# A two-layer encoder step: gathered expert rows of the early steps scaled by ScalarE and added by GpSimd

## What is computed

```
q     = (xn @ w_q).reshape(T, 8 heads, 2, 128)
sc    = q . sub_keys                    # two lists of 128 scores per head
top_s, top_i = top_k(sc, 16)            # best keys of each list
best_s, sel  = top_k(all 16*16 sums, 16); idx = pairs of keys   # choice of 16 experts
gate  = softmax(best_s)
act   = gelu(exp_u[idx] . xn)           # one dot product per chosen expert
y     = sum over heads, k of gate * act * exp_v[idx]
```

## Time and profile before

| what | value |
|---|---|
| median of 3 runs | 3265.97 us |
| the profiled execution's own time | 3254.12 us |
| its span, first to last instruction | 3252.3 us |
| granted TensorE clock, mean | 0.935 of full |
| PE busy | 2958.9 us (91%) |
| DVE busy | 2473.6 us (76%) |
| ACT busy | 811.2 us (25%) |
| POOL busy | 1056.1 us (32%) |
| DMA | 1042.99 MB, mean 321 GB/s |
| chain that ended last | PE 40%, DMA 40%, DVE 11%, issue 7% |

### The profile page before, as it was taken

The page is one execution under the profiler, slowest core; times in us unless marked ns, Lnnn a source line. Parts: engine busy times, 40 slices in busy tenths (PEclk is TensorE's granted clock), DMA queues, the critical chain, the costliest instruction groups (busy, mean ns, idle before and its releaser), DMA issues.

```text
span 3252.3 us, 46708 instructions
## 1 busy us (share of the span) xinstructions
PE 2958.9 (91%) x17310; PEld 2582.9 (79%) x17310; DVE 2473.6 (76%) x5433; ACT 811.2 (25%) x2388; POOL 1056.1 (32%) x840
## 2 busy tenths in 40 slices
PE   6898989999999999967878978789999999999876
PEld 6797778888888888855666957678888888888755
DVE  2366799988888888877533776898888888888876
ACT  4332222212111111211354362222112111112111
POOL 4532122333333333333354321122333323333331
PEclk8999999999999999988877968889999999999988
DMA  5336778999999999999311257678999999999995
GB/s 163 96 97 246 262 273 322 360 421 422 422 422 420 415 416 421 407 422 416 131 58 52 97 194 266 229 262 311 420 421 422 422 422 418 419 417 417 406 421 200
DMA packets 159967, 1042.99 MB, mean 321 GB/s; under 512 B 18480, under 2 KB 23920, under 8 KB 44096
## 3 DMA queue, kind: packets, MB, share of 16 engines
q0 software_dynamic: 92160, 671.13, 50.8%
q1 hardware_dynamic: 63648, 357.59, 28.5%
q10 hardware_dynamic: 4000, 12.36, 1.1%
HBM read 1033.28 MB, written 7.86 MB: 320 GB/s over the span
## 4 chain that ended last, share of the span: by engine, by line
PE 40%; DMA 40%; DVE 11%; issue 7%; POOL 1%; ACT 1%; SPq 0%; DVEq 0%; ACTq 0%; POOLq 0%
DMA gata<-uvg,idxg 24%; DMA gatb<-uvg,idxg 15%; PE bank L713 11%; PE bank L516 8%; DVE acc L1600 5%; PE bank L726 4%; PE bank L503 3%; PE bank L700 3%; PE bank L505 3%; PE bank L504 3%; PE bank L602 1%; PE bank L533 1%; PE bank L860 1%; DVE gata L1592 1%; PE bank L838 1%
## 5 line engine op out<-in xcount | busy, mean ns | idle before, releaser
L726 PE MATMUL bank<-a,V 128*128 128x256 f32 x4096 | 947.8, 392 | 102.5 <-DVE a L1583 102.5
L726 PEld LDWEIGHTS bank<-a,V 128*128 128x128 f32 x4096 | 805.3, 197 | 229.0 <-issue 112.6
L713 PE MATMUL bank<-xd,U 128*128 128x256 f32 x4096 | 940.2, 389 | 0.0
L1273 POOL DMA_INDIRECT gata<-uvg,idxg x428 | 525.9, 1229 | 1236.2 <-DVE acc L1600 1176.8
L713 PEld LDWEIGHTS bank<-xd,U 128*128 128x128 f32 x4096 | 790.3, 195 | 107.7 <-issue 0.2
L1592 DVE CUSTOM_DVE_ANT_0 gata<-gata,xrow 128x1024 f32<-128x1024 f32 x428 | 522.9, 1222 | 201.7 <-DMA gata<-uvg,idxg 194.9
L1600 DVE SCALAR_TENSOR_TENSOR acc<-gata,wgt,acc 128x1024 f32<-128x1024 f32 x428 | 548.5, 1281 | 32.6 <-ACT wgt L1085 32.5
L1083 ACT ACTIVATE act<-dot 128x1 f32<-128x1 f32 x640 | 129.3, 202 | 1489.3 <-DVE dot L1592 1489.2
L1273 POOL DMA_INDIRECT gatb<-uvg,idxg x212 | 254.0, 1198 | 551.1 <-DVE acc L1600 541.9
L1592 DVE CUSTOM_DVE_ANT_0 gatb<-gatb,xrow 128x1024 f32<-128x1024 f32 x212 | 259.1, 1222 | 106.6 <-DMA gatb<-uvg,idxg 105.3
L700 PEld LDWEIGHTS bank<-B,oneA 128*128 128x128 f16 x4096 | 280.0, 150 | 18.4 <-issue 6.4
(11 more groups left out here) (193 smaller groups left out, 2516.7 us busy)
## 6 DMA issues: line engine op xcount, KB each, us to landing
U<-uvd SPq DMA_DIRECT2D x128, 1024.0 KB
V<-uvd SPq DMA_DIRECT2D x128, 1024.0 KB
raw<-lin SPq DMA_DIRECT2D x152, 512.0 KB, 3.5
gata<-uvg,idxg POOLq DMA_INDIRECT x428
hsp<-h ACTq DMA_DIRECT2D x2, 2304.0 KB, 12.4
hx<-hsp SPq DMA_DIRECT2D x2, 2304.0 KB, 16.6
gatb<-uvg,idxg POOLq DMA_INDIRECT x212
sk_g<-skT ACTq DMA_DIRECT2D x2, 1024.0 KB, 4.8
```

Source lines behind the costliest of these rows:

```text
L713: mm = pe.matmul(bank[s][:, TD * t:TD * t + TD], U[:, s, o:o + P], xd[:, k, :], start=(t == 0 and k == 0), stop=(k == DT - 1), skip_group_ ...
L726: mm = pe.matmul(bank[b][:, TD * (d % 2):TD * (d % 2) + TD], V[:, s, o:o + P], a[:, s, TD * k:TD * k + TD], start=(first and k == 0 and d ...
L1273: pool.indirect_dma_start(row(l, s), None, uvg[l], bass.IndirectOffsetOnAxis(idxg[:, s:s + 1], 0)).then_inc(g_in[s % SLOTS], 16)
```

## The change

It has four parts.

1. For all steps in front of the `hot` places (`SIDE`: 34 in layer 0, 37 in layer 1) the addition leaves DVE. ACT scales the v row in its slot by the weight (a 128x1024 Copy with a scale, in place), and POOL adds the row to `acc`, then issues the gather into that slot. DVE keeps the dot.
2. ACT's weights of those steps stand one place later in ACT's program than the dots stand in DVE's.
3. The table gets one step more at `mix`, `mid2` (layer 0), `sel2` (layer 1) and `sel3`, and two more at `sel4`. `EARLY` becomes 56 and 59; 264 and 261 steps are left for the pairs, where 269 and 265 were.
4. DVE no longer waits for `acc` to be cleared; POOL, which clears it, waits in its place.

```diff
@@ AT @@
-    [("mid1", 3), ("two", 3), ("mix", 1), *[(f"add{m}", 1) for m in range(6)], ("mid2", 2), *[(f"top{m}", 1) for m in range(8, HP)],
-     ("sel3", 3), ("sel4", 3), *[(f"hot{m}", 1 + (m % 4 == 0)) for m in range(LEAD)]],
+    [("mid1", 3), ("two", 3), ("mix", 2), *[(f"add{m}", 1) for m in range(6)], ("mid2", 3),
+     *[(f"top{m}", 1) for m in range(8, HP)], ("sel3", 4), ("sel4", 5), *[(f"hot{m}", 1 + (m % 4 == 0)) for m in range(LEAD)]],
...
-     ("sel2", 2), ("sel3", 3), ("sel4", 3), *[(f"hot{m}", 1 + (m % 4 == 0)) for m in range(LEAD)]])
+     ("sel2", 3), ("sel3", 4), ("sel4", 5), *[(f"hot{m}", 1 + (m % 4 == 0)) for m in range(LEAD)]])
+SIDE = tuple(sum(n for p, n in a if p[:3] != "hot") for a in AT)
@@ ACT: squares_of_h @@
-                        weights_at(int(norm[1] == "4"), f"add{m}")
+                        weights_at(int(norm[1] == "4"), f"add{m - 1}" if m else "mix")
@@ ACT: gmlp @@
-                        if m == 12:
+                        if m == 13:
                             weights_at(0, "mid1")
+                        if m == 2 * DT - 1:
                             weights_at(0, "two")
...
                 if grp == "d":
-                    weights_at(0, "mix")
                     squares_of_h("n2d", "outd")
@@ ACT: selection @@
                         if m == 2:
                             gate_exp(l, mid)
+                        if m == 3:
                             weights_at(l, f"mid{mid}")
@@ ACT: weight @@
+                if s < SIDE[l]:
+                    v = row(l, s)[:, D:RD]
+                    act.wait_ge(wgt_done, NSTEP * l + s + 1)
+                    act.activation(v, v, ACT.Copy, scale=wgt[:, k:k + 1]).then_inc(vw_done, 1)
@@ ACT: experts @@
                     for k in range(FIRST[l]):
                         gelu(l, n + k)
+                        if k == 0:
+                            weights_at(l, f"sel{i - 1}")
                     n += FIRST[l]
                     gate_exp(l, i)
                     gelu(l, n)
-                    weights_at(l, f"sel{i}")
                     n += 1
                 for c in DC:
                     gates_high(l, c)
+                weights_at(l, f"sel{NTC - 1}")
                 gelu(l, n)
                 weights_at(l, "hot0")
@@ ACT: attention @@
-                        weights_at(1, f"att{n}")
+                        weights_at(1, f"att{n - 1}")
@@ POOL @@
+            def axpy(l, s):
+                n = min(s // P, 2)
+                pool.wait_ge(vw_done, SIDE[0] * l + s + 1)
+                if s == 0:
+                    pool.wait_ge(acc_zero, l + 1)
+                pool.wait_ge(ax_done, NSTEP * l + s)
+                pool.tensor_tensor(acc[:, n, :], acc[:, n, :], row(l, s)[:, D:RD], ALU.add).then_inc(ax_done, 1)
...
                 for s in range(SLOTS, NSTEP):
+                    if s - SLOTS < SIDE[l]:
+                        axpy(l, s - SLOTS)
@@ DVE: gathered @@
                 dot_x(l, s)
-                if s == 0:
-                    dve.wait_ge(acc_zero, l + 1)
-                else:
+                if s > SIDE[l]:
                     axpy(l, s - 1)
```

More of the change, by code:

```diff
@@ L298, in program @@
         gsel_done = sem("gsel_done")
+        vw_done = sem("vw_done")
         acc_zero, dot_done, act_done, wgt_done, ax_done = (
```

## The result

| what | before | after |
|---|---|---|
| median of the runs on one chip (5 each) | 3261.74 us | 3284.08 us (3278.68 to 3287.6) |
| ratio, 95% interval | | 1.007 [1.005, 1.009] |
| the profiled execution's own time | 3254.12 us | 3286.9 us |
| its span | 3252.3 us | 3285.1 us |
| granted TensorE clock, mean | 0.935 | 0.927 |

The time grew by 22.3 us, 0.7%. The forecast was 3268 us and no change that can be told; the time lies inside the range of 3244 to 3292, but above the forecast's own (3257 to 3279) and at the price of rival one (3286). A growth of 2 us was forecast and one of 22 measured, with an interval that leaves out no change: that the range held the time is no merit of the forecast's mechanism.

The account below looks back on a forecast made before the run. Transfers bound the pairs, PE the stretch in front of them. Layer 0 +2.5 and layer 1 -0.5 us gave +2.0 on the profiled 3254.1, so 3256.1, or 3268 us on the median; range 3244 to 3292, the forecast's own 3257 to 3279.

Parts of the forecast that it names:

- rival one: In choices and attention, POOL additions meet DVE's two-input work more often than counted: 3286 us, chance 0.28.
- Tails: Last pairs of both layers: 9 steps fewer at 2.56 us each save 23.0 us, bounds 20 and 24.
- `mid1`, `two`: Layer 0's first norm: PE's 4.53 us wait for ACT's squares goes; root 1.3 us later, bounds -1 and +3.
- Meetings in layer 0: POOL additions delay DVE's two-input work in layer 0's norms: 3.6 us at the first, 2.4 behind `add`.
- `mid2` at nothing: Layer 0's key searches: PE's wait for a copy only moves one place later; 0 us, bounds -3 and +4.
- `top`: Layer 0's `top` places: DVE 1.28 us shorter per place until PE sets the time; -2.5 us, given back next choice.
- Hand-over to the builds: After the gates, DVE's first own addition waits for POOL's five; PE loses 8 us per layer.
- The attention: Layer 1's attention: ACT's extra scaling costs 5.2 us, DVE's vanished wait for clearing `acc` saves 3.5 us.
- the section on the price that the additions bring: A POOL addition meeting two-input DVE work costs DVE up to 2.4 us; nothing taken beside one-input key searches.
- Rival two: At the builds POOL's queue is no bound: 3248 us, or 3240 with all of DVE's time; chance 0.28.

Follow-up runs that it names:

- table alone: The kernel before with only the new table of early steps, dot and weighted addition both on DVE as before: 3256.2 us, ratio 0.9991.
- no additions: The changed kernel with POOL's additions of the early steps left out, POOL signalling at once in their place: 3230.3 us, ratio 0.9912.
- 7 clearings: The changed kernel with POOL's early additions replaced by zeros written over the used row in seven instructions: 3244.5 us, ratio 0.9959.
- three additions: The changed kernel with the old counts of early steps (51 and 55), scaling on ACT and additions on POOL kept: 3282.8 us, ratio 1.0071.
- five in quarters: The changed kernel with each POOL addition cut into four instructions of 256 columns: 3291.0 us, ratio 1.0095.
- the kernel where POOL clears in one piece: The changed kernel with POOL's early additions replaced by one instruction writing zeros over the used row: 3240.5 us, ratio 0.9949.
- the two runs with DVE additions: New table, ACT's weights at later places, POOL only gathering: DVE's weighted addition as before, 3287.3 us; ACT scaling and plain DVE addition, 3310.2 us.

## Where the prediction held and where it failed, step by step

Shifts against the kernel before, in us, each trace counted from its own first indices:

| point | change | table alone | no additions | 7 clearings |
|---|---|---|---|---|
| layer 0: last matmul of the second linear layer of d | +6.7 | +2.5 | +0.9 | +0.9 |
| first key scores of d | +10.5 | +3.6 | +0.9 | +0.9 |
| end of the key searches | +13.4 | +6.9 | +0.2 | +0.3 |
| fifth one-hot | +26.5 | +13.8 | -1.6 | +8.8 |
| layer 1: first indices | +12.4 | -2.2 | -12.6 | -1.4 |
| attention's end | +20.8 | -2.3 | -9.7 | +1.6 |
| end of the key searches | +21.0 | -2.2 | -12.8 | +0.3 |
| fifth one-hot | +33.4 | +6.1 | -16.8 | +3.1 |

- **Tails: right.** 23.0 us foreseen, 22.8 measured. The three stages of the earlier trace rows and the price of a step by bytes carry over, in every one of the kernels with the new table.
- **`mid1`, `two`: right.** PE's 4.53 us for the squares became 1.77; the products of the norm began 0.9 us later by this count (1.3 foreseen, bounds -1 and +3).
- **Meetings in layer 0: right in kind, too few.** 3.6 us for the norm behind the first linear layer: 6.0 measured (from +0.9 to +6.9 at the first matmul behind it). 2.4 for the norm behind `add`: 3.8 (+6.7 to +10.5), where the run with clearings has none. The products of the first norm met two additions and those of the second one and a half (its eight took 6.89 us, 3.26 without meetings). In a queue that never rests an addition is under way two thirds of the time: POOL was adding for 2.4 of each 3.6 us.
- **`mid2` at nothing: wrong.** +5.9 from the first to the last key scores, above the bound of +4, and +5.4 to +5.6 in the kernels whose POOL reads nothing. So no meeting on DVE is needed for it: the copy that PE waits for stands behind a table load and three weights with their rows, 6.4 us. That the weights moved one place only moved the wait. But it is not ACT's rows alone: the third step that the table adds here costs +3.6 with the table alone, and the rows with the old two steps cost +3.2.
- **`top`: right.** 2.5 us gained foreseen, 3.0 measured (+16.4 to +13.4).
- **Hand-over to the builds: right in kind, mis-sized.** 8 us foreseen per layer; between the gates' copy and the second set of operands 13.5 and 14.2 were lost. Five additions and four gathers took 19.4 us (520.98 to 540.35) for the 16.0 to 18.9 allowed, since they met dots of 3.38 and 3.40 us and gathers took 1.64. The lead that was to absorb 2 us was used up before, by a first set whose product took 2.96 us. The runs with no additions (11.5, 12.3), three additions (14.3), five clearings (17.1 to 20.1), five additions (22.4, 23.1) and five in quarters (28.4, 31.4) show the mechanism in steps.
- **The attention: wrong.** 1.7 us foreseen from ACT's excess and the wait for the clearing; 8.4 measured, 3.0 with the clearings in seven pieces. So the two terms were about right, and 5.4 us of meetings were left out, in a stretch where ACT and DVE had been busy for 14 of 15 us.

The step that failed is the section on the price that the additions bring: it counted two and a half meetings, 6 us, where 43 instructions were lengthened by 72 us, and it limited them to instructions with two SBUF inputs. Up to the fifth one-hot the forecast's terms allow 15.3 us in layer 0 (1.3 + 3.6 + 2.4 + 8) and 9.7 in layer 1 (5.2 - 3.5 + 8); 26.5 and 21.0 were measured, 22.5 more. With them the forecast's +2.0 becomes +24.5; the two profiled executions lie 25.4 apart, counted from their first indices, and the medians 22.3. The excess is in four terms: the hand-overs (5.5 and 6.2), the attention (6.7), `mid2` (5.9) and the norms of layer 0 (3.8), and `mid1`, `top` and the choices give some back (-0.4, -3.0, and -0.4 and -1.9). The forecast ruled this out only by a chance of 0.28 for rival one, which named the mechanism of the meetings and, at 3286 us, came near the time; its point (four meetings more than counted) was passed in layer 0 alone. Its sum did not come about as it was made up, though: it put 18 us on the choices, but from the end of the key searches to the gates' second copy nothing was lost, so DVE's relief made up for the meetings there. Rival two fell for the reason given against it: the strict order of the additions.

## What to carry to other kernels

- Before work moves from DVE to POOL, its price is not POOL's time but what DVE loses while POOL reads: here DVE was relieved of 91 us and lengthened by 72. Count how much of the time POOL will be reading, and multiply by the DVE work beside it that reads two SBUF inputs or is of a kind that such a queue held up here (column scalings and casts); don't take the number of meetings from one example.
- An addition that others wait for in strict order costs its queue's whole length at the point where the order passes to another engine. And a weight may be made late only for an engine on which nobody waits.
- Early steps are worth their tail's price only where the front has room. Where DVE and PE are full, 9 steps cost in front what they save behind (22 us for 23), and a window that seems to have 9 of 101 us to spare is no proof of room.

## What was not expected of the hardware

**One-input instructions are held up too, even by an engine that only writes.** In the attention DVE scales S_d by a column (one SBUF input of 128x128 or 128x256). Shortest, median and longest in ns, first the kernel where POOL clears in one piece, then the change:

```profile
L1738 DVE TENSOR_SCALAR S_d<-S_d,rin x32: 278/348/2039, 1888.0 to 1951.0; 128x128 f32<-128x128 f32 x16, 128x256 f32<-128x256 f32 x16
```

```profile
L1738 DVE TENSOR_SCALAR S_d<-S_d,rin x32: 274/347/2403, 1920.5 to 1986.8; 128x128 f32<-128x128 f32 x16, 128x256 f32<-128x256 f32 x16
```

Dots are the other way round: no dot of layer 0's front was lengthened by a clearing, and eight by more than 0.5 us by an addition. In layer 1 three dots took 1.71 us, each right behind a scaling that a clearing held up. In one piece the clearing of rows held up scalings of 128x128 (1.5 to 1.9 us) and a cast of 128x128 in layer 1 (2.56). The longest scaling, 2.04 us, and a cast in layer 0 (2.65) stood beside the clearing of `acc` (2.67 us), and so they do in the kernels without additions and with seven pieces. With seven pieces no scaling was held up by a clearing of rows. The Trainium skill, "SBUF — State Buffer", section "Who interferes with whom", has both: an instruction with two SBUF inputs contends with a GpSimd instruction that reads, not with one that only writes, and copies, casts and `tensor_scalar` in their two-port modes contend with GpSimd as such. The traces agree with the first part by layer 0's dots, 1.23 us at most beside clearings and 3.40 beside additions, and with the second by the scalings of 1.5 to 2.04 us, though no trace shows in which mode these ran. The prediction had used the first part and passed over the second.

**POOL's instructions overlap at their ends.** Four quarters of an addition took 2.77 us where one whole took 2.35, not 4 x 0.90; seven clearings 2.05 where one took 1.82. Cutting costs 0.04 to 0.14 us per piece.

**The stretch from 104 to 156 us has two courses** with the same code: 280 matmul records at a granted clock of 0.91 or 239 to 257 at 0.74 to 0.78, some 7 us apart in the first copy of indices (5 with 0.78), and both courses are found with the change's POOL code and without it. Both are means over the two levels of 1.2 and 2.4 GHz. What decides between them was not tried.

Left open: how the 52 us divide between reads (some 23 to 31) and queue, since the kernel without reads had a period 0.33 us shorter than the change, and the run in quarters shows that the queue's price is not linear; and what ACT's scaling by itself costs in the change, for which the two runs with DVE additions were no measure.
